# The experts' up product as one pass of 512 columns, with the first transposes of its output placed after those of the next rows

## The reference

```python
def expert_block(args):
    xb_i, e = args
    h = jax.nn.silu(xb_i @ w_gate[e]) * (xb_i @ w_up[e])
    return h @ w_down[e]
```

## Time and profile before

| what | value |
|---|---|
| three runs, median (lowest to highest) | 2058.55 us (2058.2 to 2062.52) |
| profiled execution, first to last instruction | 2054.1 us |
| PE busy over the span | 1895.9 us, 92% |
| DVE busy | 1034.9 us, 50% |
| ACT busy | 832.3 us, 41% |
| POOL busy | 283.8 us, 14% |
| expert stage, first transpose of x to the last down matmul | about 1258 to 1997 us |
| DMA, mean over the span | 154 GB/s |

### The profile page before, as it was taken

One profiled execution on the slowest core, in us unless ns is written; L12 is line 12 of the kernel. 1 busy time (PEld: TensorE's weight loads), 2 busy tenths in 40 slices (PEclk: granted clock), 3 DMA queues, 4 the chain that ended last, 5 costly groups with the idle time before them and its releaser, 6 DMA issues. The chain is left out here.

```text
span 2054.1 us, 28746 instructions
## 1 busy us (share of the span) xinstructions
PE 1895.9 (92%) x9892; PEld 1600.8 (78%) x9893; DVE 1034.9 (50%) x2051; ACT 832.3 (41%) x1564; POOL 283.8 (14%) x388
## 2 busy tenths in 40 slices
PE   6999999999999999999997764999999999999980
PEld 5788888888878888888885543888888888888870
DVE  4644455544454544555444654454456454546434
ACT  4333333333343333333323553444446454446423
POOL 2000000010000010000100202222222222222223
PEclk9999999999999999999997886999999999999995
DMA  6332333323342223522334575585566576656428
GB/s 213 123 100 85 139 140 132 103 92 135 123 145 96 90 83 131 173 77 95 103 123 166 169 250 168 149 268 162 155 224 218 169 264 191 184 174 215 142 53 340
DMA packets 173306, 316.24 MB, mean 154 GB/s; under 512 B 9757, under 2 KB 92701, under 8 KB 173226
## 3 DMA queue, kind: packets, MB, share of 16 engines
q1 hardware_dynamic: 155754, 255.07, 36.0%
q0 software_dynamic: 15120, 51.59, 10.1%
q10 hardware_dynamic: 2352, 8.52, 1.0%
HBM read 266.09 MB, written 49.07 MB: 153 GB/s over the span
## 5 line engine op out<-in xcount | busy, mean ns | idle before, releaser
L751 DVE TENSOR_TENSOR wl<-raw,wh 128x512 fp32r<-128x512 f32 x440 | 274.3, 685 | 207.2 <-ACT wh L573 205.3
L1597 PE MATMUL bank<-gu_hi,ex_hi 128*128 128x256 f32 (+1 forms) x960 | 310.5, 323 | 4.5 <-DVE gu_lo L1507 4.5
L60 PE MATMUL bank<-xT_hi,wh 128*128 128x512 f32 x768 | 301.0, 392 | 10.6 <-ACT ext L711 7.0
L1599 PE MATMUL bank<-gu_hi,ex_lo 128*128 128x256 f32 (+1 forms) x960 | 307.1, 320 | 0.0
L1598 PE MATMUL bank<-gu_lo,ex_hi 128*128 128x256 f32 (+1 forms) x960 | 306.9, 320 | 0.0
L62 PE MATMUL bank<-xT_hi,wl 128*128 128x512 f32 x768 | 299.4, 390 | 0.0
L61 PE MATMUL bank<-xT_lo,wh 128*128 128x512 f32 x768 | 299.3, 390 | 0.0
L573 ACT ACTIVATE wh<-raw 128x512 fp32r<-128x512 f32 x440 | 240.2, 619 | 99.5 <-PE bank L1140 49.9
L1597 PEld LDWEIGHTS bank<-gu_hi,ex_hi 128*128 128x128 f32 x960 | 183.2, 191 | 23.9 <-DVE gu_lo L1507 6.5
L1599 PEld LDWEIGHTS bank<-gu_hi,ex_lo 128*128 128x128 f32 x960 | 183.2, 191 | 13.3
L1598 PEld LDWEIGHTS bank<-gu_lo,ex_hi 128*128 128x128 f32 x960 | 183.5, 191 | 12.5
(11 more groups left out here) (239 smaller groups left out, 3258.0 us busy)
## 6 DMA issues: line engine op xcount, KB each, us to landing
raw<-in_w_in SPq DMA_DIRECT2D x70, 1024.0 KB
raw_gate_up<-in_w_gate SPq DMA_DIRECT2D x16, 2048.0 KB, 8.4
raw_gate_up<-in_w_up SPq DMA_DIRECT2D x16, 2048.0 KB, 13.4
raw_d<-in_w_down SPq DMA_DIRECT2D x16, 2048.0 KB, 13.0
raw<-in_w_out SPq DMA_DIRECT2D x20, 1024.0 KB
raw<-in_w_up_pool SPq DMA_DIRECT2D x20, 512.0 KB
raw<-in_w_up_gmlp SPq DMA_DIRECT2D x20, 512.0 KB
h<-in_x_prompt SPq DMA_DIRECT2D x16, 512.0 KB, 5.2
```

What stands on the lines that cost most here:

```text
L60: nc.tensor.matmul(out, lh, rh, start=(i == 0), stop=False)
L751: lo = lambda out, x, hi: tt(out, x, hi.bitcast(F32), ALU.subtract)
L1597: nc.tensor.matmul(out, a[0][:, ka, :], w[0][:, kw, cols], start=(n == 0), stop=False)
L1599: return nc.tensor.matmul(out, a[1][:, ka, :], w[0][:, kw, cols], start=False, stop=(n == total - 1))
```

## The change

The up product goes into one bank, 24 matmuls of 512 columns in both kinds of block, like the gate product. `u1_done` disappears; DVE waits for `gu_done` and then computes both halves of `hid` in a row. In a first block DVE's `down(0)` moves ahead of that wait. On PE `hidden_transposed(0)` moves from the middle of the second half of the up product to behind `rows_of_x`, directly ahead of the down product. ACT's code is as before.

```diff
-    bankG, bankU, bankY = psum[0], psum[1:3], psum[3:5]
+    bankG, bankU, bankY = psum[0], psum[1], psum[3:5]
...
                     tt(sg[:, :], bankG[:, :], sg[:, :], ALU.mult)
                     dve.drain()
-                    dve.wait_ge(u1_done, j + 1)
-                    tt(hid[:, 0:256], bankU[0][:, 0:256], sg[:, 0:256], ALU.mult).then_inc(hid_ok, 1)
                     down(0)
+                    dve.wait_ge(gu_done, j + 2)
+                    tt(hid[:, 0:256], bankU[:, 0:256], sg[:, 0:256], ALU.mult).then_inc(hid_ok, 1)
+                    tt(hid[:, 256:512], bankU[:, 256:512], sg[:, 256:512], ALU.mult).then_inc(hid_ok, 1)
                     dve.wait_ge(hT_hi, 2 * j + 1)
                     hidden_low(0)
-                    dve.wait_ge(gu_done, j + 2)
-                    tt(hid[:, 256:512], bankU[1][:, 0:256], sg[:, 256:512], ALU.mult).then_inc(hid_ok, 1)
                     down(1)
...
-                    early = 5 if first else 0
-                    up = lambda c, k: accumulate(bankU[c][:, 0:256], xT, k, gu, KD + k,
-                                                 slice(c * 256, (c + 1) * 256), k, KD)
...
                     for k in range(KD):
                         pe.wait_ge(e_lo, SPLITS * e + KD + k + 1)
-                        last = up(0, k)
-                        if k < early:
-                            up(1, k)
-                    last.then_inc(u1_done, 1)
-                    for k in range(early, KD):
-                        last = up(1, k)
-                        if k == (6 if first else 4):
-                            pe.wait_ge(hid_ok, 2 * j + 1)
-                            hidden_transposed(0)
+                        last = accumulate(bankU[:, :], xT, k, gu, KD + k, slice(0, HALF), k, KD)
                     last.then_inc(gu_done, 1)
                     rows_of_x(16 * j + 32)
+                    pe.wait_ge(hid_ok, 2 * j + 1)
+                    hidden_transposed(0)
                     pe.wait_ge(y_read, 2 * j + 4)
```

More of the change, by code:

```diff
@@ L1336, in phase_three @@
         ex_hi, ex_lo = sem("ex_hi"), sem("ex_lo")
-        g_done, u1_done, sg_ok, hid_ok = (sem(n) for n in ("g_done", "u1_done", "sg_ok", "hid_ok"))
+        g_done, sg_ok, hid_ok = (sem(n) for n in ("g_done", "sg_ok", "hid_ok"))
         gu_done = sem("gu_done")
```

## The result

The changed kernel takes 2093.1 us (median; the kernel before beside it 2059.9), a ratio of 1.016 with a 95% interval of 1.014 to 1.018. Forecast was 2094. The profiled execution's span grew from 2054.1 to 2088.9 us, by 34.8 us.

What follows compares the result with a forecast made beforehand. PE's stream was taken to bound the expert stage. A net loss of 0.98 us in 24 later blocks (+23.5) and 0.74 in 16 first blocks (+11.8) made +35 us on 2058.55: median 2094, range 2083 to 2110.

Steps and rivals of the forecast that it cites:

- The up pass: Up product on PE as 24 matmuls of 512 columns takes 5.44 us: gain 0.53 in later blocks, 0.56 in first.
- The rival that rested on a faster pass: Up product's 512-column matmuls stream faster than the gate's, under 0.186 us each; at half of 0.227, 1985 us; 2 in 100.
- The bare chain: From first x transpose to down product, hidden's chain lies uncovered: 2.30 us; loss 1.51 in later blocks, 1.30 in first.
- The last link: From the start of DVE's hT_lo to PE's down product: 0.65 us, 0.42 instruction and 0.23 taking up.
- One link: Start of hidden's transposes on PE: after the x transposes (X+0.79) or when hid is seen (X+0.84), taken as X+0.82.
- What else moves: Side effects, such as dn_lo order and third-round waits in first blocks: costed at nothing, upper end 4 us.
- the 1.74 us gap of the earlier trace: Idle in the projection stage, followed by matmuls 0.31 then 0.23 apart at full clock; spoke against a falling clock.
- The swing between the two levels: Rival: PE's clock falls after each block's rest of about 1.1 us, costing 62 us more, about 2156; 8 in 100.
- The rival of the covered wait: Down product's wait for hT_lo stays hidden behind the x transposes, only gains remain: 25 us faster, 2034; 3 in 100.

Runs made afterwards that it cites:

- The placement alone: Kernel before, up product still in two halves; only the first transposes of hidden moved behind the transposes of x: 2106.8 us, ratio 1.0224.
- the constant: Changed kernel with the down product reading two constant tiles instead of transposed hidden, so not waiting for hT_lo: 2060.2 us, ratio 1.0007.
- the products of `hT_hi` first: Changed kernel with the down product's first slice starting with the four products that need only hT_hi, asking for hT_lo after them: 2079.3 us, ratio 1.0099.
- The first experiment: Kernel before with only the first transposes of hidden moved behind the transposes of x, up product still in halves: 2106.8 us, ratio 1.0224.

## Why the prediction was right

- The up pass: forecast 0.53 and 0.56 us a block, measured 0.52 and 0.54. The wide pass runs like the gate product. Of the gain, 0.23 us is the two transposes that left the pass; the prediction took the two effects as one, which changes nothing in its sum. In the Trainium skill, "TensorE: Matmul & The Clock Gate", section "Back-to-back issue gap", a stream of weight load and matmul pairs is given about 131 ns per matmul at 512 columns; here the 48 matmuls of gate and up product start 0.227 us apart (1306.97 to 1317.63 in 47 steps), and the measurement decides. The rival that rested on a faster pass is out.
- The bare chain: forecast 2.30 behind the x transposes, measured 2.23 in later and 2.37 in first blocks. Link by link in a later block: hid 0.20 (forecast 0.19), transposes 0.87 (0.82), hT_hi 1.29 (1.23), hT_lo 1.71 (1.65), and then 0.52 to the down product (0.65). The last link was sized from first blocks and holds there (0.67 in the row above), not in later ones, where PE starts 0.10 behind the end of `hT_lo`; there it made up for 0.06 too little before it. So the closeness of the total is in part luck: the loss was 0.07 too high in each of 24 later blocks and 0.07 too low in each of 16 first ones, -1.7 and +1.1 us, which nearly cancel. The placement alone, the constant and the products of `hT_hi` first show that this chain is the cause.
- One link was right for the wrong reason: the prediction let hidden or the x transposes set the start of the transposes of hidden, nearly together. The first experiment shows the x transposes alone: 0.87 with hidden long ready.
- What else moves: no wait of PE for `gu_lo` or `dn_lo` was added, as forecast, and DVE now waits for ACT's `hT_hi` of the first pair in all 40 blocks (before in 24). The down product of a first block is 5.81 us from its first to its last start, 5.82 before: even, as reckoned.
- The granted clock was 1.00 in every 100 us from 1300 to 2000 us, as before (from 1258 to 1300 us it was 0.84, before 0.85), with a rest of about 1 us in each block, as the 1.74 us gap of the earlier trace rows let expect. The swing between the two levels of which the Trainium skill speaks ("TensorE: Matmul & The Clock Gate", section "A second HAM failure mode: psum-queue depth-cycling") is not seen in that stretch.
- The rival of the covered wait had a wrong price. It took 25 us of gain if the wait vanished; the kernel whose down product does not wait for the chain gains nothing (1.0007), because the transposes of hidden still stand bare in PE's stream (0.22 a later block) and because in first blocks the down weights' split, which ACT begins only behind `hT_hi`, is late next (17 us).

## What to carry to other kernels

Before moving an instruction to fuse two passes, write down what its result feeds and what the bounding engine has to do meanwhile: here 0.5 us a block was saved in the passes, of which 0.3 by the width, and 1.4 us of cover given away. A long pass in place of two short ones also makes its consumers start together at its end, so look for independent work to put there first. And when a wait is taken away, price the wait behind it, and look whether it hangs on the same chain through another engine's written order: three times here the split of the down weights, behind `hT_hi` on ACT, took a part of the gain.

## What the runs showed that was not expected

- PE takes up the down product 0.52 us behind the start of hT_lo in later blocks and 0.66 in first blocks, in each of the 24 and 16 blocks, though DVE's instruction is 0.42 long in both and the order of PE's instructions around it is the same. The cause stays open. Where the down product begins with what needs only `hT_hi`, it starts 0.53 behind the start of `hT_hi` in both kinds of block.
- The eight x transposes hold PE for 0.79 us when a matmul of 512 columns follows them and for 0.87 when another transpose does.
- The second pair of transposes, taken out of the down product, shortened it by 0.24 us in a later block (5.56 to 5.33 from its first to its last start), more than the 0.15 that the starts around it suggested; in a first block it shortened it by 0.15 (5.81 to 5.66). The first pair, taken out of an up product in halves, shortened that by 0.23.
